# Hybrid attention and MoE block on one core: split rows of the merge made per chunk, router products placed later

## The reference, cut to what matters

```
merged = sigmoid(g_a) * (y_a @ w_branch_a) + sigmoid(g_b) * (y_b @ w_branch_b)   # [512, 1024]
h      = x + merged @ w_out                                                     # [512, 1024]
xn     = rmsnorm(h, g_ffn)
scores = sigmoid(xn @ w_router)                   # [512, 64], then top 4 of 8 groups, top 8 experts
h      = h + sum over chosen experts of w_e * ((silu(xn @ w_gate[e]) * (xn @ w_up[e])) @ w_down[e])
           + (silu(xn @ ws_gate) * (xn @ ws_up)) @ ws_down
```

## Time and profile before

| what | value |
|---|---|
| median of 3 runs | 1203.27 us (1201.78 to 1203.87) |
| profiled execution, its time | 1204.84 us |
| profiled execution, its span | 1203.0 us |
| busy share of PE, DVE, ACT, POOL | 93%, 39%, 23%, 24% |
| mean granted TensorE clock | 0.969 |
| DMA, mean over the span | 255 GB/s |
| bytes read and written in memory | 289.21 MB and 26.21 MB |

### The profile page before, as it was taken

How to read it: one execution, slowest core, us unless ns; L and a number is a source line. 1 busy time by engine, 2 the same in 40 slices (tenths; PEclk the granted TensorE clock), 3 DMA queues, 4 the chain that set the end, 5 groups by cost and what they waited for, 6 DMA issues and landing times.

```text
span 1203.0 us, 19007 instructions
## 1 busy us (share of the span) xinstructions
PE 1114.7 (93%) x7561; PEld 652.4 (54%) x7562; DVE 470.1 (39%) x1044; ACT 275.4 (23%) x634; POOL 284.9 (24%) x212
## 2 busy tenths in 40 slices
PE   4999999999998989988999899999998889998796
PEld 3887777767776879654333334334343333432374
DVE  5335555545546543553224312212221121110786
ACT  3104333333335320011111111111111111111623
POOL 4542434333333430001111211111211111110032
PEclk8999999999998989978999999999999999999898
DMA  9921132221113403639899999999999999998761
GB/s 278 247 71 36 48 76 55 67 56 53 54 36 104 124 28 123 254 154 404 340 422 421 422 403 422 422 414 416 407 419 410 405 409 409 404 391 308 300 298 70
DMA packets 118040, 306.20 MB, mean 255 GB/s; under 512 B 21792, under 2 KB 79808, under 8 KB 91968
## 3 DMA queue, kind: packets, MB, share of 16 engines
q1 hardware_dynamic: 105712, 270.88, 58.9%
q0 software_dynamic: 12240, 34.09, 7.1%
HBM read 289.21 MB, written 26.21 MB: 262 GB/s over the span
## 4 chain that ended last, share of the span: by engine, by line
PE 68%; SPq 12%; DMA 9%; issue 6%; DVE 3%; POOLq 1%; POOL 1%; DVEq 0%; ACT 0%
PE bank L453 16%; PE bank L1439 15%; PE bank L1463 7%; DMA sb_gate_up<-in_w_up 7%; SPq L975 6%; PE bank L1059 4%; SPq L979 4%; PE bank L1047 4%; PE bank L462 3%; PE bank L486 3%; PE bank L517 3%; PE bank L1084 3%; PE bank L499 2%; PE bank L1429 2%; DMA sb_ple_early<-in_w_ple 2%
## 5 line engine op out<-in xcount | busy, mean ns | idle before, releaser
L1439 PE MATMUL bank<-sb_gate_up,sb_xgT 128*32 128x512 f32 (+2 forms) x2144 | 302.8, 605 | 23.3 <-DMA sb_gate_up<-in_w_up 23.3
L1439 PEld LDWEIGHTS bank<-sb_gate_up,sb_xgT 128*32 128x32 f32 (+2 forms) x2144 | 95.7, 118 | 198.5 <-issue 195.3
L453 PE MATMUL bank<-sb_x_hl,sb_w_hl 128*128 128x512 f32 x768 | 201.2, 406 | 0.0
L453 PEld LDWEIGHTS bank<-sb_x_hl,sb_w_hl 128*128 128x128 f32 x768 | 138.5, 190 | 43.7 <-issue 16.0
L1463 PE MATMUL bank<-sb_down,sb_work 128*32 128x512 f32 (+2 forms) x1072 | 154.7, 602 | 4.2 <-DMA sb_down<-in_w_down 3.0
L1510 POOL DMA_INDIRECT expert_rows<-sb_rows_out,sb_work x42 | 43.2, 1028 | 463.9 <-DVE sb_rows_out L1582 463.9
L241 POOL TENSOR_TENSOR sb_w_hl<-sb_r,sb_w_hl 128x1024 fp32r<-128x1024 f32 x54 | 132.4, 2457 | 58.5 <-ACT sb_w_hl L1167 45.9
L1592 DVE TENSOR_TENSOR sb_work<-sb_work,bank 128x256 f32<-128x256 f32 x42 | 17.8, 423 | 277.4 <-ACT sb_work L1628 277.4
L1463 PEld LDWEIGHTS bank<-sb_down,sb_work 128*32 128x32 f32 (+2 forms) x1072 | 47.0, 117 | 80.3 <-issue 77.3
L235 POOL CAST sb_w_hl<-sb_r 128x1024 fp32r<-128x1024 f32 x35 | 37.7, 1077 | 205.5 <-PE bank L453 158.1
L1628 ACT ACTIVATE sb_work<-bank 128x256 f32<-128x256 f32 x42 | 16.2, 387 | 304.5 <-PE bank L1439 304.5
(11 more groups left out here) (250 smaller groups left out, 1267.6 us busy)
## 6 DMA issues: line engine op xcount, KB each, us to landing
sb_gate_up<-in_w_gate SPq DMA_DIRECT2D x64, 1024.0 KB, 19.4
sb_gate_up<-in_w_up SPq DMA_DIRECT2D x64, 1024.0 KB, 28.4
sb_down<-in_w_down SPq DMA_DIRECT2D x64, 1024.0 KB, 29.1
sb_r<-in_w_in SPq DMA_DIRECT2D x34, 512.0 KB, 3.9
sb_rows<-expert_rows SPq DMA_DIRECT2D x6, 2048.0 KB, 16.3
sb_r<-in_w_out SPq DMA_DIRECT2D x8, 512.0 KB, 3.9
sb_rows<-expert_rows SPq DMA_DIRECT2D x4, 1024.0 KB, 7.8
sb_h<-in_x SPq DMA_DIRECT2D x4, 512.0 KB, 8.4
```

Source lines behind the costliest of these rows:

```text
L453: last = nc.tensor.matmul(out[:, :], w6_hl[:, slot_at[n], zw, k, :], x_hl[:, zx, k, :], start=k + i == 0, stop=k == KD - 1 and i == 2)
L1439: last = nc.tensor.matmul(bank[BH][rows, :], xgT[:, k, rows], gate_up[slot_of[r]][:, :, k, :], start=k == 0, stop=k == KD - 1)
```

## The change

It gives the two parts of the merged rows homes of their own: `m_hi` in the place of `y` (tile-major, chunk k of tile t at `[:, t, k, :]`), `m_lo` in the place of `mT` itself. ACT copies chunk m right behind its merge, and DVE subtracts chunk m - 1 behind the merge of chunk m, and chunk 7 last. The PE starts the first quarter with chunks 0 to 6 of all four tiles once seven chunks are split, and then adds chunk 7 for all four. The router product of tile t - 2 stands between quarters 2 and 3 of tile t; that of tile 2 follows the last transposes.

```
+        m_hi = sb("m_hi", Y0, [P, NT, KD, P], F32R)
+        m_lo = sb("m_lo", G0, [P, KD, S], F32R)
...
-            def out_proj(t, q):
+            def out_proj(t, q, chunks_=range(KD)):
                 lo = (2, 4, 0, 2)[q]
-                n = 0
-                for k in range(KD):
-                    if t == q == 0:
-                        pe.wait_ge(M["mt_lo"], k + 1)
-                    for zx, zw in PASSES:
-                        last = nc.tensor.matmul(bank[t][:, (q % 2) * 256:(q % 2 + 1) * 256], x_hl[:, zx, k, t * P:(t + 1) * P],
-                                                w6_hl[:, lo:lo + 2, zw, k, :], start=n == 0, stop=n == 3 * KD - 1)
-                        n += 1
-                last.then_inc(M["wo_done"], 1)
+                for k in chunks_:
+                    for i, (zx, zw) in enumerate(PASSES):
+                        part_of_m = m_lo[:, k, t * P:(t + 1) * P] if zx else m_hi[:, t, k, :]
+                        last = nc.tensor.matmul(bank[t][:, (q % 2) * 256:(q % 2 + 1) * 256], part_of_m,
+                                                w6_hl[:, lo:lo + 2, zw, k, :], start=k + i == 0, stop=k == KD - 1 and i == 2)
+                if k == KD - 1:
+                    last.then_inc(M["wo_done"], 1)
...
             pe.wait_ge(s_split, WO_PIECE + 4)
-            pe.wait_ge(M["merged"], KD)
-            for q in range(2):
-                for t in range(NT):
-                    out_proj(t, q)
+            pe.wait_ge(M["mt_lo"], KD - 1)
+            for t in range(NT):
+                out_proj(t, 0, range(KD - 1))
+            pe.wait_ge(M["mt_lo"], KD)
+            for t in range(NT):
+                out_proj(t, 0, range(KD - 1, KD))
+            for t in range(NT):
+                out_proj(t, 1)
             pe.wait_ge(s_split, WO_PIECE + KD)
             for t in range(NT):
                 pe.wait_ge(M["h_done"], t + 1)
-                for q in (2, 3):
-                    out_proj(t, q)
+                out_proj(t, 2)
+                if t == 2:
+                    pe.wait_ge(s_wr, 32)
+                if t >= 2:
+                    router(t - 2)
+                out_proj(t, 3)
                 if t:
                     transpose_xn(t - 1)
-                    if t == 1:
-                        pe.wait_ge(s_wr, 32)
-                    router(t - 1)
             pe.wait_ge(M["h_done"], NT + 1)
             pe.wait_ge(s_ws, 32)
             shared_up(0)
             transpose_xn(3)
+            router(2)
             router(3)
...
# ACT, middle_scalar, in the loop over m behind round_piece and gate
-            act.wait_ge(M["merged"], KD)
-            for k in range(KD):
-                nc.scalar.copy(x_hl[:, 0, k, :], mT[:, k, :]).then_inc(M["mt_hi"], 1)
+                act.wait_ge(M["merged"], m + 1)
+                nc.scalar.copy(m_hi[:, :, m, :], mT[:, m, :].rearrange("p (t n) -> p t n", t=NT)).then_inc(M["mt_hi"], 1)
...
# DVE, middle_vector
+            def rest_of_m(k):
+                dve.wait_ge(M["mt_hi"], k + 1)
+                nc.vector.tensor_tensor(m_lo[:, k, :].rearrange("p (t n) -> p t n", t=NT), mT[:, k, :].rearrange("p (t n) -> p t n", t=NT),
+                                        m_hi[:, :, k, :].bitcast(F32), ALU.subtract).then_inc(M["mt_lo"], 1)
...
                 nc.vector.tensor_tensor(mT[:, m, :], gateT[:, m, :], gateT[:, KD + m, :], ALU.add).then_inc(M["merged"], 1)
-            for k in range(KD):
-                dve.wait_ge(M["mt_hi"], k + 1)
-                nc.vector.tensor_tensor(x_hl[:, 1, k, :], mT[:, k, :], x_hl[:, 0, k, :].bitcast(F32), ALU.subtract).then_inc(M["mt_lo"], 1)
+                if m:
+                    rest_of_m(m - 1)
+            rest_of_m(KD - 1)
```

## The result

The changed kernel takes 1194.91 us in the median of 5 runs (1194.41 to 1197.05), the kernel before 1202.0 us in 5 (1200.55 to 1203.87). The ratio is 0.9945, 95% interval 0.9934 to 0.9956: 6.6 us faster, with 5.3 to 7.9 us in the interval. The forecast was 3.5 us and a range down to 1197.7 us. The sign and both places of the gain were right; the size was about half of what came.

A forecast was written before the change was run, and what follows sets the result against it. PE work up to the shared products bounds the start of the DMA-bound expert-weight stream. An earlier start (0.4 us) plus router gaps (3.1 us) give 3.5 us, from 1203.27 to 1199.8 us; range 1197.7 to 1202.3 us.

The forecast's parts named there:

- The chain: Merge to shared products: the PE is the chain; reaching its last shared product earlier moves the expert-weight stream by as much.
- The rival in which the stream swallows the gain: Experts' stage: 480 us of transfers drift by over 3.5 us or meet an unfree slot; 1203.3 us, chance 0.09.
- The start of the out-projection: Behind the merge: the PE starts 0.7 us earlier, at about 431.15 us; what is saved is one ACT copy.
- its cause in DVE's order: Merge's end: chunk 6's subtraction stands behind chunk 7's add, so no more than 0.7 us is saved.
- the four gaps of 3.1 us: Before each tile's router product: the PE's waits for copies to `xn2T`, 0.81 + 3 x 0.77 us, all go.
- shared products covering the normalised rows: Before tile 3's transposes: 6.92 us of `shared_up(0)` covers the 4.6 us wait for rows, 2.3 us to spare.
- DVE's budget: Merge loop: each 0.62 to 0.7 us subtraction fits DVE's 1.43 us idle per chunk; the rival, 1208.7 us, had chance 0.07.
- ACT's wait: Merge loop: ACT's copy waits for its chunk's merge, yet ends by 425.7 us, so the rounding at 426.36 isn't late.
- subtractions over 1.4 us: Merge loop: sign of a wrong forecast; from 1.43 us per subtraction on, DVE exceeds its idle time per chunk.
- first load near 533.5 us: Experts' stage: sign of a right forecast, SP's first load of weights, issued at 536.97 us before.
- The first term's 0.4 us: Out-projection's start at the low clock: 0.7 us earlier is worth 0.35 or 0.7 us; 0.4 us was taken.
- its lower end: Range's fast end, 1197.7 us: the case of a shorter clock dip (1198.1 us, chance 0.10) less 0.4 us.

The follow-up runs named there:

- homes alone: Kernel before with the merged rows' two parts in `m_hi` and `m_lo`, split still one block behind the merge, PE order unchanged: 1201.47 us, ratio 0.9983.
- split alone: Changed kernel with the old loop of router products, keeping the split beside the merge and the new homes: 1200.35 us, ratio 0.9975 to the kernel before.
- router alone: Kernel before with only the new router loop and `router(2)` behind `transpose_xn(3)`: 1198.58 us, ratio 0.9958.
- one step further: Changed kernel with DVE subtracting chunk 6 before the products of chunk 7: 1189.9 us, ratio 0.989 to the kernel before.

## Why the prediction was right or wrong

**Right.** The chain (PE up to the shared products, the stream of weights behind it, all moving together): the first expert's product comes at 553.24, 551.24, 549.33, 547.90, 544.79 and 537.45 us in the profiles of before, homes alone, split alone, router alone, changed, and one step further, and the rest of the span behind it is 647.8 to 649.8 us in all six. So start and end move together to within 2 us. The rival in which the stream swallows the gain fell with that. The start of the out-projection (0.7 us forecast, 0.77 measured), its cause in DVE's order, the four gaps of 3.1 us, shared products covering the normalised rows, DVE's budget and ACT's wait came as written, except that the sign "subtractions over 1.4 us" did show in one of eight, without harm. The later instants (first load near 533.5 us) can't be judged against one profile; with the clock's chance it came at 528.8 us.

**Wrong: "All four gaps go: 0.81 + 3 x 0.77 = 3.1 us".** The gaps did go, but the step took the idle time between pieces as the whole price of a stop. The router matmuls behind each stop carried 0.25 us more, 2.0 against 1.73 us. The term measured 4.2 us in the kernel with the router alone, 28.9 against 33.16 us.

**Wrong: what the new homes do to the matmuls, left at nothing.** The prediction went through the split's instructions and never through the matmuls that read it, since their number and shape stay. Their pace went from 0.1200 to 0.1167 us; over 384 matmuls that is 1.3 us, and the kernel with the homes alone has it.

**The first term's 0.4 us** for an earlier start at the low clock held. From the merge's end to the 288th matmul's end the two profiles of before took 42.1 and 42.7 us, the two of the changed kernel 40.8 and 41.4 us: 1.25 us less, of which 288 x 3.3 ns = 0.95 us are the new homes' and 0.3 us the start's. In both pairs the clock came back at the same distance from the merge's end in the two kernels (9.5 and 9.6 us in the first, 10.8 and 10.9 in the second), so that the earlier start gave about half of its 0.77 us. Measured from the restart it differs: it came 4.0 us after the restart in the first one of before, 4.9 and 6.1 us in two of the changed kernel, 2.9 us in the split alone. The Trainium skill ("TensorE: Matmul & The Clock Gate", What's actually happening) calls the window free-running; by it the return is not tied to the restart. These four profiles agree, so what one execution gets of the 0.77 us is chance.

The sum with the measured terms: 0.3 + 1.3 + 4.2 = 5.8 us, against 5.7 us in the marks and 6.6 us (5.3 to 7.9) in the runs. What is left, under 1 us, the runs can't tell from chance. The range failed because its lower end held only the clock's chance, no bound for a term that was larger than the gaps seen. A smaller part of the miss is the base: the forecast counted down from 1203.27 us, the median of three runs, and the median of five is 1202.0 us.

## What to carry to other kernels

A stop of the PE can cost more than the idle time that the chain shows, here 0.25 us on top of 0.77: compare the duration of the same group of matmuls with and without a wait before it, and add the difference. When operands get another place, time the instructions that read them too, even if their number and shape stay. When work is moved ahead so that a wait is met early, look for the last instruction in the order that still stands behind something late: here one reordered subtraction was worth as much as the whole change. And before a difference between two profiles is explained, compare stretches of untouched code; if they differ too, profile both again.

## What was not expected of the hardware

The place of the stationary rows changes the matmuls' pace: 128 x 256 matmuls follow each other every 0.1200 us with both parts in the place of `x_hl`, every 0.1178 us with one part moved and every 0.1167 us with both, at the same clock and with the same neighbours. Why the place matters is open. And the clock's first low stretch behind the router was 3.4 to 10.2 us long in twelve profiles, though the code there is the same in all; at half speed that alone is up to 3.4 us.
